# Other places for the buffers modulo 512 bytes, eight blocks of modulation weights later, and the last products in another order

## The chip, the cores and the metric

The kernel runs on one core of one Trainium2 chip, as one launch. The metric is the device time in microseconds (us). TensorE is called PE here, its weight load PEld, VectorE DVE, ScalarE ACT, GpSimd POOL, and the queue of SyncE, which issues the loads of the weights, SP.

## What is computed

Two blocks of a transformer follow each other on 256 tokens of width 1024, each with two layers, all in float32. Each layer is a mixer and a feed-forward part, and what goes into and out of both is scaled by rows that depend on the condition `c`.

```python
def swiglu(h, w1, w3, w2):
    a = jnp.einsum("btd,df->btf", h, w1)
    g = jnp.einsum("btd,df->btf", h, w3)
    return jnp.einsum("btf,fd->btd", jax.nn.silu(a) * g, w2)        # d = 1024, f = 2816
...
for layer in range(DEPTH):                                           # first block, DEPTH = 2
    shift, scale, gate = modulation(c, ada_w[layer, 0], ada_b[layer, 0])
    h = x * (1.0 + scale) + shift
    y = hybrid_mixer(h, ...)                                         # w_in, three small mixers, w_out
    x = layer_norm(DN_ALPHA * x + (1.0 + gate) * y, ...)
    shift, scale, gate = modulation(c, ada_w[layer, 1], ada_b[layer, 1])
    h = x * (1.0 + scale) + shift
    y = swiglu(h, ...) if layer % 2 == 0 else moe_swiglu(h, ...)     # 8 experts, top 2
    x = layer_norm(DN_ALPHA * x + (1.0 + gate) * y, ...)
...
for l in range(L):                                                   # second block, L = 2
    mod = (cond @ w_mod[l] + b_mod[l])[:, None, :]
    sh_a, sc_a, g_a, sh_f, sc_f, g_f = jnp.split(mod, N_MOD, axis=-1)
    h = rms_norm_2(x, norm_mix[l]) * (1 + sc_a) + sh_a
    ...                                                              # w_in, two kinds of attention
    x = x + g_a * (jnp.concatenate([o_m, o_d], axis=-1) @ w_out[l])
    h = rms_norm_2(x, norm_ffn[l]) * (1 + sc_f) + sh_f
    x = x + g_f * ((jax.nn.silu(h @ w_gate[l]) * (h @ w_up[l])) @ w_down[l])
```

## The kernel before

**Weights in blocks of 1 MB.** All large weights come in blocks of 128 partitions by 2048 float32 numbers, each one DMA of SP, into a ring of six slots (`ring`, NS = 6). `plan` is the list of the blocks in order. SP waits for a slot until the block that lay in it has been used. A feed-forward part has 33 blocks: 22 of w1 and w3 and 11 of w2. `weave` puts blocks of modulation weights (`mods`, four blocks for each of 24 pieces `(m, j)`: m is the part, j = 0, 1, 2 shift, scale and gate) between the others; `lead` and `tail` say how many blocks of the main list stay free of them at its start and end.

**Three products for one.** Each number is split into a high and a low half that PE multiplies as float32r. ACT makes the high half of a weight block (`high_halves`, `ring_hi`, L1293), DVE subtracts to get the low half into the slot itself (`low_halves`, `ring_lo`, L1990), and `product` (L510 to L513) issues three matmuls: high by high, high by low, low by high. In a row of the profile the names behind `bank<-` are first the moving operand, which streams through PE, then the stationary one, which is loaded as weights (128 columns, 512 bytes in each partition).

**Which operand is which.** In `up`, and in `feature_block` of the first mixers, the rows of activations `hh`, `hl` move (256 columns) and the weight block is stationary. In `token_block`, `project` and the output blocks it is the other way round: `hh`, `hl` (or `yl`) are stationary and the weight block moves, with 256 (168 in one block) or 512 columns. In `down` and `last_down` the units (`uh`, `ul`, which lie in `work`; in groups of odd number parts of `PTr`) are stationary and 512 columns of weights move. The eight experts run in the branch `moe_picked`: for each the picked rows are gathered into `hgh`, `hgl` (in `QK` for experts 0, 1, 3, 4, 6 and 7; for experts 2 and 5 in the buffer of `hT` and `hl`, so that the profile names it `hl`) and are stationary under 512 columns of weights, or 256 in an expert's last group.

**Modulation on DVE.** DVE multiplies and sums a modulation block in two instructions of 1024 columns (`gemv`, L1930). It does so inside `low_halves`, ahead of the split of the next block in the plan, so the place of a modulation block in the plan sets its place in DVE's order.

**The end of a feed-forward part.** `last_down` works on result blocks 9 and 10 (the last two of 11) over four output quarters `Y[t][hf]`. DVE takes each quarter as soon as its last product is done, and the next part's norm follows from there.

**Fillers.** `turn_over` issues matmuls on constants whose results nobody reads.

**Where the buffers lie.** Each buffer begins where the one before ends, at a multiple of 32 bytes. In the built program the ring begins at byte 16,512 of a partition, which is 128 modulo 512. All the buffers up to `PT` are multiples of 512 bytes long, so they begin at 128 as well: the ring, `ring_hi`, `X`, `hT`/`hl`, `hh`, `XN`, `YT`/`yl`, `PT`/`PTr`. `PT` is 17,216 bytes long, so `YK`, `QK` (with `hgh`, `hgl`), `acc`, the gates and `cst` begin at 448, and `work` (with `uh`, `ul`) at 416. Slices inside these buffers, as the products take them, are multiples of 512 bytes apart, except in the block of 168 columns.

Of the kernel before, what the change touches and what calls it, by code (L numbers as in the profile page):

```python
# [88 lines left out]
def hybrid_kernel(nc, a, out):  # L89
    ctx = ExitStack()  # L90
    with ctx:
# [19 lines left out]
        X = sb("X", [128, 2, 1024])  # L111
        hT, hl = sb_over("hT", [128, 8, 256], "hl")
        hh = sb("hh", [128, 8, 256], F32R)
        XN, xl = sb_over("XN", [128, 2, 1024], "xl")
        YT, yl = sb_over("YT", [128, 8, 256], "yl")
        PT, PTr = sb_over("PT", [128, 4304], "PTr")
        YK = sb("YK", [128, 2, 1024])
        at_qk = (nc.sbuf_base + 31) // 32 * 32
        QK = sb("QK", [128, 4, 4, 256])
        hgl2 = over("hgl", [128, 2, 8, 128], at_qk)  # L120
        hgh2 = over("hgh", [128, 2, 8, 128], at_qk + 8192)
        acc = sb("acc", [128, 3072])
        gate = [sb(f"gate{i}", [128, 1024]) for i in range(NG)]
# [3 lines left out]
        pB = sb("pB", [128, 36])  # L127
        pD = sb("pD", [128, 80])
# [4 lines left out]
        small = sb("small", [128, 2, 24])  # L133
        gmr = sb("gmr", [128, 2, 256])
# [5 lines left out]
        prmD = YKf[:, 896:1024]  # L140
        at_work = (nc.sbuf_base + 31) // 32 * 32
        work = sb("work", [128, 2560])
        Sm = work[:, 0:1536].rearrange("p (j c) -> p j c", j=4)
# [7 lines left out]
        pos = sb("pos", [128, 2], I32)  # L151
        rp2 = sb("rp2", [128, 2, 2, 8])
        mlaw = sb("mlaw", [128, 1280])
        rtr, rtl = sb_over("rtr", [128, 8, 8], "rtl")
        rth = sb("rth", [128, 8, 8], F32R)
        comb = sb("comb", [128, 2, 8])
        st2 = sb("st2", [128, 48])
        flag = sb("flag", [128, 1], I32)
        sstat = sb("sstat", [128, 96])
        lam = sb("lam", [128, 2])  # L160
# [183 lines left out]
        def put_blocks(blocks):  # L344
            for b in blocks:
                block(*b)
# [4 lines left out]
        for i, n in enumerate((0, 1, 1, 1, 1, 2, 2)):  # L351
# [7 lines left out]
        put_blocks(weave(ffn_blocks((("ffn", 0), a["ffn_w1"][0], a["ffn_w3"][0], a["ffn_w2"][0])),  # L359
                         mods((1, 2), (4, 0), (4, 1), (2, 0), (2, 1), (2, 2), (3, 0), (3, 1))))  # L360
        put_blocks(weave(win_blocks(1) + rowblocks(("wout", 1), a["w_out"][1]), mods((3, 2))))
        put_blocks(weave(ffn_blocks(*[(("moe", x), a["moe_w1"][0, x], a["moe_w3"][0, x], a["moe_w2"][0, x]) for x in range(8)]), mods((4, 2)), 6, 6))
# [25 lines left out]
        for m in range(8):  # L388
            for j in range(3):
# [5 lines left out]
                if j == 2 and m >= 6:  # L395
                    sums.setdefault(turn_of[("win2", 1, 8) if m == 6 else ("wout2", 1, 1)], []).append((m, j))
                    continue
# [81 lines left out]
        def tensor_program(pe):  # L479
# [205 lines left out]
            def last_down(s, key):  # L685

                for i in (9, 10):
                    if key[0] != "moe":
                        summed(turn_of[(*key, "w2", i)])
                for t in range(2):  # L690
                    for hf in range(2):
                        for i in (9, 10):
                            wh, wl = weights(s, *key, "w2", i)
                            g, h = divmod(i, 2)
                            if t == 0 and hf == 0:
                                pe.wait_ge(*at(s.part, *key, "u", g, h))
                            for c in range(2):
                                w = slice(1024 * c + 512 * hf, 1024 * c + 512 * hf + 512)
                                j, z = 2 * h + c, slice(128 * t, 128 * t + 128)
                                x = product(Y[t][hf][:, :], fuh[g % 2][:, j, z], ful[g % 2][:, j, z], wh[:, w], wl[:, w], False, i == 10 and c == 1)  # L700
                            names = [("use", s.part, (*key, "w2", i)), (s.part, *key, "down", i, 1)] if t and hf else []
                            if i == 10:
                                names.append((s.part, *key, "result", t, hf))
                            if names:
                                x.then_inc(*s.prod(*names))

# [478 lines left out]
            first_sum(0)  # L1185
            turn_over(Y[1][1][:, :], 20)
            first_sum(1)
# [1951 lines left out]
```

## Time and profile before

| | |
|---|---|
| three timed runs | 2095.27 us median (2092.81 to 2095.79) |
| the profiled execution | 2093.15 us, of which the span of the trace is 2091.3 us |
| PE busy | 1990.1 us (95%), 11776 matmuls |
| DVE busy | 1672.5 us (80%) |
| ACT busy | 1169.8 us (56%) |
| DMA | 554.41 MB, mean 265 GB/s |

Busy time is the time in which an engine has at least one instruction under way. Matmuls overlap, so what a matmul costs in a row of them is not its duration but the distance from its start to the next one's. The clock is the share of the full PE clock that was granted.

In order of time the span holds: the first mixer (from 37 us), the first feed-forward part (186 to 392), the second mixer (400 to 534, with the choice of the experts), the experts (541 to 1351), the third mixer (1372 to 1536), its feed-forward part (1540 to 1737), the fourth mixer (1744 to 1897) and the last feed-forward part (1900 to 2087).

### The profile page before, as it was taken

To read this page: it belongs to the slowest core of one execution; us is meant where nothing else is said; L and a number is where in the kernel's file an instruction comes from. 1 tells how busy PE (TensorE), PEld (TensorE's weight loads), DVE (VectorE), ACT (ScalarE), POOL (GpSimd) and SP (SyncE) were. 2 spreads that over 40 slices of the span, in tenths; PEclk is the share of its full clock that TensorE was granted. 3 is DMA by queue.
4 is the path that set the end of the run, shared out by engine and by line. 5 is a ranking of instruction groups with operands and counts; after the bars stand their busy time and mean duration, and the time that the engine had idled before them with its cause. 6 is when DMAs were issued, how large, how long until landed. Compare 5 with 4: busy or idle time off the path is not lost.

```text
span 2091.3 us, 28839 instructions
## 1 busy us (share of the span) xinstructions
PE 1990.1 (95%) x11776; PEld 1696.9 (81%) x11798; DVE 1672.5 (80%) x1753; ACT 1169.8 (56%) x1316; POOL 72.8 (3%) x121
## 2 busy tenths in 40 slices
PE   7999999999899999999999999898899999989999
PEld 6778899786678888887888888677689988869998
DVE  6778889887789898989889888878778887856444
ACT  3544434464677776777777777456444345654432
POOL 6001000000000000000000000000010000000000
PEclk8999999999999999999999999999899999999999
DMA  9855999645599999999999999824369994324552
GB/s 354 265 188 192 356 350 359 213 140 192 193 336 341 359 366 333 351 360 366 330 351 364 363 337 350 293 95 148 121 230 346 352 356 145 122 72 150 182 185 97
DMA packets 251211, 554.41 MB, mean 265 GB/s; under 512 B 10076, under 2 KB 75856, under 8 KB 251072
## 3 DMA queue, kind: packets, MB, share of 16 engines
q1 hardware_dynamic: 247252, 544.13, 73.7%
q0 software_dynamic: 3552, 8.29, 1.1%
q8 instruction: 96, 1.57, 0.3%
q14 instruction: 43, 0.35, 0.0%
q10 hardware_dynamic: 268, 0.07, 0.0%
HBM read 551.40 MB, written 1.05 MB: 264 GB/s over the span
## 4 chain that ended last, share of the span: by engine, by line
PE 71%; DVE 15%; ACT 7%; issue 4%; DMA 4%; SPq 0%; ACTq 0%; DVEq 0%
PE bank L511 21%; PE bank L513 21%; PE bank L512 21%; DVE ring_lo L1990 4%; ACT ring_hi L1293 3%; DVE acc L1930 2%; DMA ring<-in_ffn_w_dram 1%; PE bank L902 1%; PE bank L1110 1%; DVE work L2175 1%; DMA ring<-in_w_in_dram 1%; DMA ring<-in_ada_w_dram 1%; PE bank L539 1%; DMA ring<-in_w_gate_dram 1%; DVE st L2179 1%
## 5 line engine op out<-in xcount | busy, mean ns | idle before, releaser
L1990 DVE TENSOR_TENSOR ring_lo<-ring,ring_hi 128x2048 fp32r<-128x2048 f32 x417 | 949.2, 2285 | 251.6 <-ACT ring_hi L1293 248.9
L1293 ACT ACTIVATE ring_hi<-ring 128x2048 fp32r<-128x2048 f32 x417 | 794.8, 1912 | 473.7 <-PE bank L513 225.5
L511 PE MATMUL bank<-hh,ring_hi 128*128 128x256 f32 x1152 | 328.2, 285 | 9.8 <-DVE ring_lo L1990 8.0
L512 PE MATMUL bank<-hl,ring_hi 128*128 128x256 f32 x1152 | 326.1, 283 | 0.0
L513 PE MATMUL bank<-hh,ring_lo 128*128 128x256 f32 x1152 | 326.0, 283 | 0.0
L513 PE MATMUL bank<-ring_hi,hl 128*128 128x256 f32 (+2 forms) x768 | 236.0, 307 | 0.0
L511 PEld LDWEIGHTS bank<-hh,ring_hi 128*128 128x128 f32 x1152 | 220.9, 192 | 13.6 <-issue 7.0
L511 PE MATMUL bank<-ring_hi,hgh 128*128 128x512 f32 (+1 forms) x576 | 220.6, 383 | 7.4 <-DVE ring_lo L1990 3.0
L512 PEld LDWEIGHTS bank<-hl,ring_hi 128*128 128x128 f32 x1152 | 221.1, 192 | 0.9 <-issue 0.5
L513 PEld LDWEIGHTS bank<-hh,ring_lo 128*128 128x128 f32 x1152 | 221.0, 192 | 0.0
L511 PE MATMUL bank<-ring_hi,hh 128*128 128x256 f32 (+2 forms) x672 | 209.3, 311 | 11.8 <-DVE hl L2054 6.5
L513 PE MATMUL bank<-ring_hi,hgl 128*128 128x512 f32 (+1 forms) x576 | 216.4, 376 | 0.0
L512 PE MATMUL bank<-ring_lo,hgh 128*128 128x512 f32 (+1 forms) x576 | 216.3, 376 | 0.0
L511 PE MATMUL bank<-ring_hi,uh 128*128 128x512 f32 x496 | 199.5, 402 | 7.3 <-DVE ring_lo L1990 6.1
L512 PE MATMUL bank<-ring_lo,hh 128*128 128x256 f32 (+2 forms) x672 | 202.6, 302 | 0.0
L512 PE MATMUL bank<-ring_lo,uh 128*128 128x512 f32 x496 | 197.1, 397 | 0.0
L513 PE MATMUL bank<-ring_hi,ul 128*128 128x512 f32 x496 | 197.1, 397 | 0.0
L1930 DVE SCALAR_TENSOR_TENSOR acc<-ring,csil,acc 128x1024 f32<-128x1024 f32 x140 | 179.7, 1283 | 12.8 <-DMA ring<-in_ada_w_dram 6.8
L513 PEld LDWEIGHTS bank<-ring_hi,hl 128*128 128x128 f32 x768 | 148.4, 193 | 6.6
L511 PEld LDWEIGHTS bank<-ring_hi,hh 128*128 128x128 f32 x672 | 130.9, 195 | 25.8 <-issue 15.8
L511 PEld LDWEIGHTS bank<-ring_hi,hgh 128*128 128x128 f32 x576 | 108.2, 188 | 33.5 <-issue 6.6
L512 PEld LDWEIGHTS bank<-ring_lo,hh 128*128 128x128 f32 x672 | 131.1, 195 | 4.6 <-issue 0.7
(427 smaller groups left out, 2815.2 us busy)
## 6 DMA issues: line engine op xcount, KB each, us to landing
ring<-in_moe_w_dram SPq DMA_DIRECT2D x264, 1024.0 KB, 5.3
ring<-in_ada_w_dram SPq DMA_DIRECT2D x48, 1024.0 KB, 7.4
ring<-in_w_mod_dram SPq DMA_DIRECT2D x48, 1024.0 KB, 7.6
ring<-in_w_in_dram SPq DMA_DIRECT2D x40, 1024.0 KB, 5.5
ring<-in_ffn_w_dram SPq DMA_DIRECT2D x33, 1024.0 KB, 5.7
ring<-in_w_gate_dram SPq DMA_DIRECT2D x22, 1024.0 KB, 5.1
ring<-in_w_up_dram SPq DMA_DIRECT2D x22, 1024.0 KB, 5.3
ring<-in_w_down_dram SPq DMA_DIRECT2D x22, 1024.0 KB, 5.1
```

The source lines that it names most:

```text
L511: pe.matmul(ps, xh, wh, start=first, stop=False)
L512: pe.matmul(ps, xh, wl, start=False, stop=False)
L513: return pe.matmul(ps, xl, wh, start=False, stop=last)
L539: x = pe.matmul(R2.of("gatesum", 0, h)[:, :], bc(csil[:, 2 * p + k:2 * p + k + 1], [128, 128]), w[:, k, 512 * h:512 * h + 512], start=p == ...
L902: x = pe.matmul(Y[t][h][:, :], YT[:, 2 * i + k, 128 * t:128 * t + 128], w[:, c:c + 512], start=first and k == 0, stop=False)
L1110: x = pe.transpose(ps[:, 128 * c:128 * c + 128], U[:, 128 * c:128 * c + 128], ident)
L1293: act.activation(ring_hi[i % NH][:, 0:z], ring[n % NS][:, 0:z], ACT.Copy).then_inc(*s.hi(("hi", home(s, i), i)))
L1930: x = dve.scalar_tensor_tensor(v, w[:, k, :], csil[:, col:col + 1], v, ALU.mult, ALU.add)
L1990: dve.tensor_tensor(ring_lo[n % NS][:, 0:z], ring[n % NS][:, 0:z], hi, ALU.subtract).then_inc(*s.lo(("lo", home(s, i), i)))
L2175: dve.tensor_tensor(S, R.of(*A, "scores", i, c)[:, 0:384], mask, ALU.add).then_inc(*vec(("free", *A, "scores", i, c)))
L2179: dve.tensor_reduce(mx[:, 1:2], S[:, 128:384], AXX, ALU.max).then_inc(*vec())
```

## The change

1. The buffers are allocated in another order. `QK`, `work`, `YK`, `acc`, the gates and `cst` now begin at 128 modulo 512, as `XN`, `YT`, `PT` and the ring still do; `hh` and `hT`/`hl` begin at 320.
2. Modulation piece (3, 1), four blocks, moves from the first feed-forward part to the second mixer, and piece (7, 2), four blocks, from the third feed-forward part to the last; the sum of (7, 2) on PE (L580, four matmuls) moves with it from the fourth mixer into the last feed-forward part.
3. `last_down` does three of the four quarters of block 9 before it turns to block 10.
4. The filler in the first 40 us has 15 matmuls, not 20.

```diff
@@ buffers
-        hT, hl = sb_over("hT", [128, 8, 256], "hl")
-        hh = sb("hh", [128, 8, 256], F32R)
         XN, xl = sb_over("XN", [128, 2, 1024], "xl")
-        YT, yl = sb_over("YT", [128, 8, 256], "yl")
-        PT, PTr = sb_over("PT", [128, 4304], "PTr")
-        YK = sb("YK", [128, 2, 1024])
         at_qk = (nc.sbuf_base + 31) // 32 * 32
         QK = sb("QK", [128, 4, 4, 256])
...
+        at_work = (nc.sbuf_base + 31) // 32 * 32
+        work = sb("work", [128, 2560])
+        YT, yl = sb_over("YT", [128, 8, 256], "yl")
+        PT, PTr = sb_over("PT", [128, 4304], "PTr")
+        rtr, rtl = sb_over("rtr", [128, 8, 8], "rtl")
+        rp2 = sb("rp2", [128, 2, 2, 8])
+        hh = sb("hh", [128, 8, 256], F32R)
+        hT, hl = sb_over("hT", [128, 8, 256], "hl")
+        small = sb("small", [128, 2, 24])
...
+        YK = sb("YK", [128, 2, 1024])
         acc = sb("acc", [128, 3072])
...
@@ plan
-                         mods((1, 2), (4, 0), (4, 1), (2, 0), (2, 1), (2, 2), (3, 0), (3, 1))))
-        put_blocks(weave(win_blocks(1) + rowblocks(("wout", 1), a["w_out"][1]), mods((3, 2))))
+                         mods((1, 2), (4, 0), (4, 1), (2, 0), (2, 1), (2, 2), (3, 0))))
+        put_blocks(weave(win_blocks(1) + rowblocks(("wout", 1), a["w_out"][1]), mods((3, 1), (3, 2)), 2, 2))
...
-                             mods((5, 2), (6, 0), (6, 1), (6, 2), (7, 0), (7, 1), (7, 2)) if l == 0 else []))
+                             mods((5, 2), (6, 0), (6, 1), (6, 2), (7, 0), (7, 1)) if l == 0 else mods((7, 2)), 2, 1 if l == 0 else 12))
...
@@ last_down
-                for t in range(2):
-                    for hf in range(2):
-                        for i in (9, 10):
...
+                early = [(0, 0), (0, 1), (1, 0)]
+                for i, t, hf in [(9, *q) for q in early] + [(10, 0, 0), (10, 0, 1), (9, 1, 1), (10, 1, 0), (10, 1, 1)]:
...
@@ start
-            turn_over(Y[1][1][:, :], 20)
+            turn_over(Y[1][1][:, :], 15)
```

PE's order at the end of the first feed-forward part, before; each row stands for six products (its own and the five left out below it), block 9 has the units `uh` and block 10 those in `PTr`, and the bank gives the quarter:

```order
L511 MATMUL bank0<-ring_hi0,uh_62 128x512
...
L511 MATMUL bank0<-ring_hi1,PTr_58 128x512
...
L511 MATMUL bank1<-ring_hi0,uh_62 128x512
...
L511 MATMUL bank1<-ring_hi1,PTr_58 128x512
...
L511 MATMUL bank2<-ring_hi0,uh_62 128x512
...
L511 MATMUL bank2<-ring_hi1,PTr_58 128x512
...
L511 MATMUL bank3<-ring_hi0,uh_62 128x512
...
L511 MATMUL bank3<-ring_hi1,PTr_58 128x512
```

And now:

```order
L511 MATMUL bank0<-ring_hi0,uh_63 128x512
...
L511 MATMUL bank1<-ring_hi0,uh_63 128x512
...
L511 MATMUL bank2<-ring_hi0,uh_63 128x512
...
L511 MATMUL bank0<-ring_hi1,PTr_59 128x512
...
L511 MATMUL bank1<-ring_hi1,PTr_59 128x512
...
L511 MATMUL bank3<-ring_hi0,uh_63 128x512
...
L511 MATMUL bank2<-ring_hi1,PTr_59 128x512
...
L511 MATMUL bank3<-ring_hi1,PTr_59 128x512
```

Six products of block 9 stood ahead of the first that needs block 10; now eighteen do.

DVE's order in the second mixer, before, from the second half of the row norm on (`XN<-YT,pA,XN` is the convolution, `acc` a modulation block, `ring_lo` the split of a weight block):

```order
L2024 TENSOR_TENSOR X<-XN,QK 128x1024
L2026 TENSOR_TENSOR X<-X,QK 128x1024
L1990 TENSOR_TENSOR ring_lo_50<-ring,ring_hi 128x2048
L2237 SCALAR_TENSOR_TENSOR XN<-YT,pA,XN 128x256 x6
...
L1930 SCALAR_TENSOR_TENSOR acc<-ring,csil,acc 128x1024 x2
L1990 TENSOR_TENSOR ring_lo_52<-ring,ring_hi 128x2048
L2237 SCALAR_TENSOR_TENSOR XN<-YT,pA,XN 128x256 x6
L1990 TENSOR_TENSOR ring_lo_53<-ring,ring_hi 128x1344
L2237 SCALAR_TENSOR_TENSOR XN<-YT,pA,XN 128x256 x6
```

And now:

```order
L2023 TENSOR_TENSOR X<-XN,QK 128x1024
L2025 TENSOR_TENSOR X<-X,QK 128x1024
L1929 SCALAR_TENSOR_TENSOR acc<-ring,csil,acc 128x1024 x2
L1989 TENSOR_TENSOR ring_lo_53<-ring,ring_hi 128x2048
L2236 SCALAR_TENSOR_TENSOR XN<-YT,pA,XN 128x256 x6
...
L1929 SCALAR_TENSOR_TENSOR acc<-ring,csil,acc 128x1024 x2
L1989 TENSOR_TENSOR ring_lo_49<-ring,ring_hi 128x2048
L2236 SCALAR_TENSOR_TENSOR XN<-YT,pA,XN 128x256 x6
L1929 SCALAR_TENSOR_TENSOR acc<-ring,csil,acc 128x1024 x2
L1989 TENSOR_TENSOR ring_lo_51<-ring,ring_hi 128x1344
L2236 SCALAR_TENSOR_TENSOR XN<-YT,pA,XN 128x256 x6
```

Two more modulation blocks stand ahead of the splits of the fifth and the seventh input block. A third stands in the same way ahead of the eighth.

DVE's order at the end of the same mixer, before, ahead of the split of the output blocks:

```order
L2067 TENSOR_TENSOR yl<-YT,hh 128x512 x2
L1930 SCALAR_TENSOR_TENSOR acc<-ring,csil,acc 128x1024 x2
L1990 TENSOR_TENSOR ring_lo_54<-ring,ring_hi 128x2048
L1990 TENSOR_TENSOR ring_lo_49<-ring,ring_hi 128x2048
L1990 TENSOR_TENSOR ring_lo_50<-ring,ring_hi 128x2048
L2074 TENSOR_TENSOR XN<-bank,gate 128x512
```

And now:

```order
L2066 TENSOR_TENSOR yl<-YT,hh 128x512 x2
L1929 SCALAR_TENSOR_TENSOR acc<-ring,csil,acc 128x1024 x4
L1989 TENSOR_TENSOR ring_lo_54<-ring,ring_hi 128x2048
L1989 TENSOR_TENSOR ring_lo_49<-ring,ring_hi 128x2048
L1989 TENSOR_TENSOR ring_lo_50<-ring,ring_hi 128x2048
L2073 TENSOR_TENSOR XN<-bank,gate 128x512
```

The fourth extra block is summed here, so that four instructions of `acc` stand ahead of the split, not two.

## Rows read from the trace of the kernel before

**Rows 1.** The page, sections 1 and 4: busy time by engine; the chain of waits.

```profile
PE 1990.1 (95%) x11776; PEld 1696.9 (81%) x11798; DVE 1672.5 (80%) x1753; ACT 1169.8 (56%) x1316; POOL 72.8 (3%) x121
...
PE 71%; DVE 15%; ACT 7%; issue 4%; DMA 4%; SPq 0%; ACTq 0%; DVEq 0%
```

**Rows 2.** Windows over five stages: PE, PEld, DVE, ACT, POOL busy, clock, DMA, GB/s.

```profile
185.70:392.30 206.60, 198.60 (x1361) 183.68 (x1362) 181.53 (x142) 81.22 (x68) 6.71 (x10) 0.98 0.87 316
399.70:533.90 134.20, 125.55 (x846) 103.43 (x849) 105.59 (x208) 78.82 (x141) 6.60 (x10) 1.00 0.45 151
541.00:1351.00 810.00, 793.03 (x3740) 646.61 (x3741) 712.27 (x478) 573.92 (x427) 0.00 (x0) 1.00 0.98 347
1539.60:1737.30 197.70, 192.22 (x1327) 178.40 (x1326) 164.06 (x124) 81.32 (x70) 1.44 (x2) 0.99 0.87 314
1899.60:2087.00 187.40, 187.39 (x1320) 176.19 (x1320) 93.07 (x63) 75.10 (x59) 0.00 (x0) 1.00 0.47 155
```

**Rows 3.** Timeline of PE in the last feed-forward part: start, duration, instruction.

```profile
1945.78 0.40 PE L511 MATMUL bank<-ring_hi,uh 128*128 128x512 f32 x1
...
1956.97 0.28 PE L511 MATMUL bank<-hh,ring_hi 128*128 128x256 f32 x1
...
1980.00 0.40 PE L511 MATMUL bank<-ring_hi,PTr 128*128 128x512 f32 x1
...
1990.90 0.28 PE L511 MATMUL bank<-hh,ring_hi 128*128 128x256 f32 x1
```

**Rows 4.** Timeline of PE in the experts: 36 products with 256 columns, twice.

```profile
634.89 0.37 PE L511 MATMUL bank<-ring_hi,hgh 128*128 128x256 f32 x1
...
639.07 0.45 PE L511 MATMUL bank<-ring_hi,uh 128*128 128x512 f32 x1
...
834.71 0.36 PE L511 MATMUL bank<-ring_hi,hl 128*128 128x256 f32 x1
...
839.11 0.40 PE L511 MATMUL bank<-ring_hi,uh 128*128 128x512 f32 x1
```

**Rows 5.** Lines of PE by form: count, busy us, mean ns.

```profile
L511 PE MATMUL bank<-hh,ring_hi 128*128 128x256 f32 x1152 | 328.2, 285 | 9.8 <-DVE ring_lo L1990 8.0 <-ACT hT L1348 1.4 <-DVE hl L2054 0.3
L511 PE MATMUL bank<-ring_hi,uh 128*128 128x512 f32 x496 | 199.5, 402 | 7.3 <-DVE ring_lo L1990 6.1 <-DVE ul L2697 1.0
L511 PE MATMUL bank<-ring_hi,hgh 128*128 128x512 f32 x480 | 193.4, 403 | 7.4 <-DVE ring_lo L1990 3.0 <-DVE hgl L2648 1.8 <-ACT QK L1754 1.5
L511 PE MATMUL bank<-ring_hi,hh 128*128 128x256 f32 x544 | 159.6, 293 | 10.2 <-DVE hl L2054 6.5 <-DVE ring_lo L1990 3.0 <-ACT PT L1440 0.8
L511 PE MATMUL bank<-ring_hi,hl 128*128 128x512 f32 x160 | 64.1, 400 | 2.4 <-DVE ring_lo L1990 1.2 <-ACT QK L1754 1.1
L511 PE MATMUL bank<-ring_hi,hgh 128*128 128x256 f32 x96 | 27.2, 283 | 0.0
```

**Rows 6.** Timeline of PE before two last result blocks, then a window's clock.

```profile
379.72 0.79 PE L511 MATMUL bank<-ring_hi,PTr 128*128 128x512 f32 x1 [3.97 <-DVE ring_lo L1990]
...
1725.92 0.51 PE L511 MATMUL bank<-ring_hi,PTr 128*128 128x512 f32 x1 [3.21 <-DVE ring_lo L1990]
...
379.00:386.00 7.00, 6.28 (x15) 4.97 (x16) 6.90 (x7) 1.24 (x2) 0.00 (x0) 0.52 0.48 152
```

**Rows 7.** Timeline of DVE and PE at the end of the second mixer.

```profile
498.57 2.60 DVE L1930 SCALAR_TENSOR_TENSOR acc<-ring,csil,acc 128x1024 f32<-128x1024 f32 x2
501.09 4.49 DVE L1990 TENSOR_TENSOR ring_lo<-ring,ring_hi 128x2048 fp32r<-128x2048 f32 x2
...
503.52 0.47 PE L511 MATMUL bank<-ring_hi,hh 128*128 128x512 f32 x1 [1.43 <-DVE ring_lo L1990]
```

**Rows 8.** Who waited for whom in the experts; then the page's GB/s by slice.

```profile
ACT ring_hi L1293 <- PE bank L513: 154.0, 149, 2.9
ACT ring_hi L1293 <- DMA ring<-in_moe_w_dram: 2.1, 3, 0.9
...
GB/s 354 265 188 192 356 350 359 213 140 192 193 336 341 359 366 333 351 360 366 330 351 364 363 337 350 293 95 148 121 230 346 352 356 145 122 72 150 182 185 97
```

More of the change, by code:

```diff
@@ L121, in hybrid_kernel @@
         hgh2 = over("hgh", [128, 2, 8, 128], at_qk + 8192)
+        at_work = (nc.sbuf_base + 31) // 32 * 32
[7 more added lines that the diff above has]
+        small = sb("small", [128, 2, 24])
+        rth = sb("rth", [128, 8, 8], F32R)
+        st2 = sb("st2", [128, 48])
+        sstat = sb("sstat", [128, 96])
+        pD = sb("pD", [128, 80])
+        YK = sb("YK", [128, 2, 1024])
         acc = sb("acc", [128, 3072])
@@ L127, in hybrid_kernel @@
         pB = sb("pB", [128, 36])
-        pD = sb("pD", [128, 80])
         lnc = sb("lnc", [128, 8])
@@ L132, in hybrid_kernel @@
         csil = sb("csil", [128, 16])
-        small = sb("small", [128, 2, 24])
         gmr = sb("gmr", [128, 2, 256])
@@ L140, in hybrid_kernel @@
         prmD = YKf[:, 896:1024]
-        at_work = (nc.sbuf_base + 31) // 32 * 32
-        work = sb("work", [128, 2560])
         Sm = work[:, 0:1536].rearrange("p (j c) -> p j c", j=4)
@@ L151, in hybrid_kernel @@
         pos = sb("pos", [128, 2], I32)
-        rp2 = sb("rp2", [128, 2, 2, 8])
         mlaw = sb("mlaw", [128, 1280])
-        rtr, rtl = sb_over("rtr", [128, 8, 8], "rtl")
-        rth = sb("rth", [128, 8, 8], F32R)
         comb = sb("comb", [128, 2, 8])
-        st2 = sb("st2", [128, 48])
         flag = sb("flag", [128, 1], I32)
-        sstat = sb("sstat", [128, 96])
         lam = sb("lam", [128, 2])
@@ L395, in hybrid_kernel @@
                 if j == 2 and m >= 6:
-                    sums.setdefault(turn_of[("win2", 1, 8) if m == 6 else ("wout2", 1, 1)], []).append((m, j))
+                    sums.setdefault(turn_of["win2", 1, 8] if m == 6 else turn_of["ffn2", 1, "w1", 5, 0], []).append((m, j))
                     continue
@@ L689, in last_down @@
                         summed(turn_of[(*key, "w2", i)])
-                for t in range(2):
-                    for hf in range(2):
-                        for i in (9, 10):
[L693 to L705, printed above, removed]
+                early = [(0, 0), (0, 1), (1, 0)]
+                for i, t, hf in [(9, *q) for q in early] + [(10, 0, 0), (10, 0, 1), (9, 1, 1), (10, 1, 0), (10, 1, 1)]:
+                    wh, wl = weights(s, *key, "w2", i)
+                    g, h = divmod(i, 2)
+                    if t == 0 and hf == 0:
+                        pe.wait_ge(*at(s.part, *key, "u", g, h))
+                    for c in range(2):
+                        w = slice(1024 * c + 512 * hf, 1024 * c + 512 * hf + 512)
+                        j, z = 2 * h + c, slice(128 * t, 128 * t + 128)
+                        x = product(Y[t][hf][:, :], fuh[g % 2][:, j, z], ful[g % 2][:, j, z], wh[:, w], wl[:, w], False, i == 10 and c == 1)
+                    names = [("use", s.part, (*key, "w2", i)), (s.part, *key, "down", i, 1)] if t and hf else []
+                    if i == 10:
+                        names.append((s.part, *key, "result", t, hf))
+                    if names:
+                        x.then_inc(*s.prod(*names))
             def attention(A, heads):
```

## The prediction

> **What bounds the kernel now.** I read the page first. PE is busy 95% of the span, and the chain of waits lies on PE for 71% of it [rows 1], so what shortens a run of matmuls shortens the kernel, unless something waits right behind. Then the windows by stage [rows 2]. In the last feed-forward part PE is busy for all of its 187.4 us. The first has 206.6 - 198.6 = 8.0 us idle, the third 197.7 - 192.2 = 5.5, and in both DMA is busy 0.87 of the time. The experts are busy 793 of 810 us with DMA at 0.98. In the second mixer PE (125.6) and DVE (105.6) share 134.2 us. The timeline gives the pace, from the first matmul of a run to the first behind it [rows 3]: 48 matmuls with `uh` (at 416) as the stationary operand and 512 columns take 1956.97 - 1945.78 = 11.19 us, 233.1 ns each; 48 with `PTr` (128) take 1990.90 - 1980.00 = 10.90, 227.1 each; between them 192 with 256 columns of `hh` (128) over a weight block (128) take 23.03, 119.9 each. In the experts [rows 4] 36 matmuls of 256 columns with `hgh` at 448 take 4.18 us, 116.1 each, and the same 36 of an expert whose rows lie at 128 take 4.40, 122.2 each. So the place modulo 512 counts: at 512 columns the stationary operand wants 128 (6.0 ns less than at 416), at 256 columns it wants 448 (6.1 less than at 128). In both pairs the moving operand begins at 128.
>
> **The addresses, product by product.** Counts are those of one of the three products of a kind, times 3 [rows 5].
> Units, 416 to 128 under 512 columns: 496 x 3 = 1488 matmuls, of them 8 experts x 11 blocks x 4 x 3 = 1056 in the experts, 432 in three feed-forward parts. At 6.0 ns: 6.3 us and 2.6 us (0.9 a part).
> Gathered rows, 448 to 128: 480 x 3 = 1440 at 512 columns save 8.6 us; 96 x 3 = 288 at 256 columns lose 1.8. Experts 2 and 5 go from 128 to 320 (160 x 3 = 480 at 512 columns): between nothing and the 6.0 ns that 416 costs, 0 to +2.9 us; I take +1.1. The experts save 6.3 + 8.6 - 1.8 - 1.1 = 12.0.
> `hh`, `hl` as the moving operand, 128 to 320 over a weight block at 128, 256 columns: 1152 x 3 = 3456, of them 352 x 3 = 1056 in each feed-forward part and 288 in the first two mixers. No row has a moving operand at 320. What the cheap row has is a distance: moving 128, stationary 448, that is 192 modulo 512. Moving 320 over stationary 128 is again 192. If the distance decides, each saves 6.1 ns; if the stationary place alone does, nothing; and 6.1 more is the other end, since one such move did cost that at 512 columns. I take -6.1, the row with the same distance: 6.4 us a part, 19.3 for three, 1.8 in the mixers.
> `hh`, `hl` as the stationary operand at 320 (token and projection blocks): 544 x 3 = 1632, distance 320, in no row. Between -6.1 and +6.1 ns, 10 us either way; I take half the gain, -5.0 us.
>
> **What of that is on the path.** In the feed-forward parts all of it. In the mixers PE alternates with DVE and ACT: half of 1.8 + 5.0, so 3.4. In the experts ACT waits 154 us for PE to release a tile and 2.1 us for DMA [rows 8], so PE sets the pace there, but the loads are near. 268 blocks of 1.049 MB are 281 MB; at 366 GB/s, the best slice of the page [rows 8], they need 768 us against 810 now. There is room for 12 us; since DVE is busy 712 of 810 and gives PE hiccups, I take 85%: 10.2.
>
> **Modulation blocks.** The first feed-forward part loads 61 blocks, not 65. At its 316 to 359 GB/s four blocks are 12 to 13 us of DMA. It waits for loads (8.0 us idle), so its idle goes to about 1: -7.0. In the third part, 57 blocks for 61, 5.5 goes to about 1: -4.4. Both figures include step 3. In the last part four more loads find DMA 0.47 busy and DVE 93 of 187: nothing, and if that cover went, 4 x 2.6 = 10.4 us. The sum of (7, 2) is four matmuls on PE in one place or the other: nothing.
> The second mixer pays. Each block is two `acc` instructions, 2.60 us together [rows 7], four blocks 10.4 us on DVE, which was busy 105.6 of 134.2. One stands where PE waits already: PE got its low half at 503.52, with 1.43 us idle and DVE without a gap ahead of it [rows 7], so that one costs its full 2.6. The other three stand ahead of splits in the middle, behind them the convolution, the rotations and the softmax that PE needs; but there ACT and PE make DVE wait too. Bounds 0 and 7.8 for the three; I take 1.4, as 28 us of DVE's stage are idle. Sum +4.0. SP only issues four loads more, at DMA 0.45.
>
> **The last products.** PE waits 3.97 and 3.21 us for the low half of block 10 [rows 6], six matmuls into the end. Now eighteen stand ahead of it, 12 x 0.227 = 2.7 us more cover; that wait is part of the idle counted. After it 30 matmuls follow, not 42. The wait in the first part also pulls the clock down: granted 0.52 from 379 to 386 [rows 6], 42 matmuls at 1.2 GHz for most of 7 us, so about 3.4 us lost. With a wait of a microsecond I expect the clock to hold: -3.0. The quarters now come in two pairs, so DVE's norm ends a bit closer behind the last: -1.0 over two parts. Filler 20 to 15: DVE is late anyway there: 0.
>
> **Sum.** -19.3 (up) -2.6 (units in three parts) -3.4 (mixers) -10.2 (experts) -7.0 -4.4 (idle) -3.0 (clock) -1.0 (norm) +4.0 (second mixer) = -46.9. The profiled execution took 2093.15, 2.1 below the median of the runs. 2095.3 - 46.9 = 2048.4, so 2048.
>
> **Rivals.**
> A, the stationary place alone decides: nothing from `hh` at 320. Without 19.3 and 3.4 the gain is 24.2: 2071. For it: both pairs of rows change the stationary operand alone. Against: the sign turns between 256 and 512 columns, which a rule on the stationary operand by itself does not give.
> B, the gain in the experts is lost since DMA, at 0.98, or DVE, at 0.88, is late next, and the first part stays on its loads (3 us less gained): -46.9 + 13 = -34: 2061.
> C, the addresses do nothing: only idle, clock, norm and mixer remain, -11.4: 2084. For it nothing in the rows, against it [rows 3, 4].
> This is what the Trainium skill says, in "SBUF — State Buffer", section "Who interferes with whom": PE has two read ports, one for the moving operand and one for LDWEIGHTS, independent of each other, and "PE and ACT never wait on anyone". The trace disagrees: 233.1 against 227.1 ns with only the stationary buffer's place different.
> D, slower: `hh` at 320 costs 6.1 ns more, not less, in both of its roles. 3456 + 1632 = 5088 matmuls are +31.0 us. The rest gives 24.2, so +6.8: 2102. It decides from 24.2 / 5088 = 4.8 ns a matmul on. For it: at 512 columns leaving 128 did cost 6. Against: at 256 it gained.
>
> **How the numbers follow.** Forecast 0.64, A 0.16, B 0.11, C 0.03, D 0.06. The forecast's own range is 2038 to 2058 (second mixer 0 to 10, stationary role either way). The range has to reach A and B: 2036 to 2076 leaves out C, D and the forecast's lower edge. A measurement of this kernel can tell about 0.2%, 4 us, from no change. Only D is slower: 0.06. Between D and C a part of either could end within 4 us: 0.02, taken from C. Faster 0.92.
>
> **What would show it.** In the last feed-forward part: 192 up products in 22.0 us (114 ns) if I am right, 23.0 under A, 24.2 under D; every 48 result products in 10.9 us; the part 187.4 - 7.3 = 180 us long. The experts: `hgh` runs at 227 ns with 512 columns and 122 with 256; about 800 us long; ACT's wait for the experts' loads above 10 us would be B. First part: idle at most 2 us, clock 1.00 at its end. Second mixer: `acc` x4 ahead of the output blocks' splits and PE's wait there 4 us, not 1.43. I am wrong if `up` stays at 120, or if the second mixer takes over 8 us more.

## The result and the profile after

Four runs of the changed kernel took 2073.2 us in the median (2071.79 to 2075.66), four of the kernel before beside them 2094.04 (2091.84 to 2095.79). The ratio is 0.9902, 95% interval 0.9885 to 0.9919: 1.0% faster, 20.8 us. Forecast was a gain of 46.9. The sign was right and 2073.2 lies in the stated 2036 to 2076, near its far end and near rival A's 2071; the size was not right.

The page of after, the rows that answer to [rows 1]:

```profile
PE 1971.2 (95%) x11793; PEld 1687.0 (81%) x11793; DVE 1672.0 (81%) x1753; ACT 1170.6 (56%) x1316; POOL 72.0 (3%) x121
...
PE 70%; DVE 17%; ACT 7%; issue 4%; DMA 2%; SPq 0%; ACTq 0%; DVEq 0%
```

PE is busy 18.9 us less, as long as the span became shorter (2072.5 for 2091.3). DVE has more of the chain, 17% for 15. Windows of after (columns as in [rows 2]: PE, PEld, DVE, ACT, POOL busy, clock, DMA share, GB/s), from the first feed-forward part to the last in the same order, the second mixer cut where [rows 2] cuts it:

```profile
184.20:377.20 193.00, 190.66 (x1361) 177.46 (x1362) 166.90 (x125) 80.91 (x67) 6.72 (x10) 1.00 0.89 323
390.90:534.80 143.90, 128.30 (x851) 105.73 (x849) 114.94 (x215) 77.66 (x138) 6.55 (x10) 0.98 0.48 166
542.00:1341.00 799.00, 781.81 (x3736) 645.79 (x3736) 710.81 (x475) 571.95 (x425) 0.00 (x0) 1.00 0.98 351
1534.00:1720.90 186.90, 185.80 (x1327) 173.89 (x1326) 152.78 (x113) 80.56 (x66) 1.44 (x2) 1.00 0.86 312
1883.60:2068.20 184.60, 184.52 (x1324) 173.02 (x1324) 102.30 (x71) 76.23 (x61) 0.00 (x0) 1.00 0.53 180
```

The first part's idle fell from 8.0 to 2.3 us, the third's from 5.5 to 1.1. The first part now ends at 377.2 and the second mixer begins at 390.9, where before it was 392.3 and 399.7: a gap of 14 us stands where one of 8 was. The second mixer is 9.7 us longer, with DVE busy 9.4 us more and a clock of 0.98. The experts are 8.6 us shorter, at DMA 0.98 as before.

The last part, PE's timeline (start, duration), as [rows 3]: the start of 192 up products, the first result product behind them, the start of the next 192 and the first behind those.

```profile
1938.48 0.28 PE L511 MATMUL bank<-hh,ring_hi 128*128 128x256 f32 x1
...
1961.09 0.39 PE L511 MATMUL bank<-ring_hi,PTr 128*128 128x512 f32 x1
...
1971.97 0.28 PE L511 MATMUL bank<-hh,ring_hi 128*128 128x256 f32 x1
...
1994.59 0.39 PE L511 MATMUL bank<-ring_hi,uh 128*128 128x512 f32 x1
```

192 up products take 22.61 us, 117.8 ns each: neither the 114 of the forecast nor the 120 of rival A. The 48 result products take 10.88 us, 226.7 each, as forecast. But the first 384 up products of the same part (1883.61 to 1927.59) go at 114.5. So `up` has two paces in one trace, with the same operands at the same places. In the experts, as [rows 4], 36 products of 256 columns with `hgh` now at 128 take 4.40 us, 122.2 each, as forecast:

```profile
634.80 0.36 PE L511 MATMUL bank<-ring_hi,hgh 128*128 128x256 f32 x1
...
639.20 0.40 PE L511 MATMUL bank<-ring_hi,uh 128*128 128x512 f32 x1
```

The stages, in us, from the start of the first product of one to that of the next in the timeline of each kernel (a feed-forward part ends at its last result product, its gap reaches to the first product of what follows). The columns behind after are experiments of the next section. Each column is one execution, and single stages differ by a few us without a cause in the edit: after and fill_last1 (next section) have the same instructions up to the first part, which starts at 184.3 in one and at 188.2 in the other.

| | before | after | places_only | order_only | back31 | old_last | hh128 | hh448 | fill_r64 |
|---|---|---|---|---|---|---|---|---|---|
| start of the first part | 185.8 | 184.3 | 187.7 | 187.1 | 185.0 | 185.3 | 186.9 | 187.8 | 185.4 |
| first part | 206.2 | 192.6 | 203.3 | 194.6 | 201.4 | 194.5 | 194.2 | 192.3 | 191.9 |
| gap behind it | 7.7 | 14.0 | 7.7 | 13.7 | 11.3 | 8.0 | 13.6 | 13.1 | 13.3 |
| second mixer | 141.4 | 151.1 | 141.1 | 151.0 | 141.1 | 152.9 | 151.3 | 154.0 | 151.4 |
| experts | 806.9 | 798.3 | 798.4 | 806.9 | 798.5 | 798.8 | 798.2 | 799.4 | 798.1 |
| third part | 197.4 | 186.6 | 191.5 | 189.7 | 185.7 | 188.7 | 189.2 | 187.2 | 183.4 |
| last part | 187.4 | 184.5 | 184.2 | 189.1 | 186.0 | 184.5 | 188.3 | 186.1 | 183.9 |

### The profile page after: what moved, and what is told of

Same layout as the page of the kernel before. It is cut to its first block, busy times and chain, and to the rows that moved or that the text cites. A ratio compares the mean times of both kernels' runs of the same rounds, so it can differ in the third digit from the quotient of the medians.

```text
span 2072.5 us, 28850 instructions
## 1 busy us (share of the span) xinstructions
PE 1971.2 (95%) x11793; PEld 1687.0 (81%) x11793; DVE 1672.0 (81%) x1753; ACT 1170.6 (56%) x1316; POOL 72.0 (3%) x121
## 4 chain that ended last, share of the span: by engine, by line
PE 70%; DVE 17%; ACT 7%; issue 4%; DMA 2%; SPq 0%; ACTq 0%; DVEq 0%
PE bank L511 21%; PE bank L512 20%; PE bank L513 20%; DVE ring_lo L1989 5%; ACT ring_hi L1292 3%; DVE acc L1929 2%; PE bank L901 1%; DMA ring<-in_ada_w_dram 1%; PE bank L1109 1%; DVE XN L2073 1%; PE bank L539 1%; DVE work L2174 1%; DMA ring<-in_ffn_w_dram 1%; PE bank L593 1%; PE bank L498 1%
```

## The experiments

My theory after the result: the gain comes from the buffers' places alone; the order of the work is worth nothing in sum, since the gap behind the first part and the second mixer give back what the parts gain. The rival: the two halves add as they were forecast, each smaller. For `up`: the distance between the operands decides, but a run has two paces at this distance; the rival, that the moving operand at 320 has a pace of its own and something else in the kernel disturbs it.

**places_only.** The kernel before with the allocation of the changed one:

```diff
-        hT, hl = sb_over("hT", [128, 8, 256], "hl")
-        hh = sb("hh", [128, 8, 256], F32R)
...
+        rp2 = sb("rp2", [128, 2, 2, 8])
+        hh = sb("hh", [128, 8, 256], F32R)
+        hT, hl = sb_over("hT", [128, 8, 256], "hl")
```

> The kernel before with the buffers at the places of the changed kernel; blocks, last products and filler as before. By the trace of the changed kernel, `up` gains 2 to 3 ns a product, not 6.1, and the experts 9 us; with units and mixers that is 18 to 22 us: about 2074 when before is 2094, and the order of the work gave nothing. By the rival, that the order gave its 11 of idle and clock and the places the rest, 10: about 2084. If the prediction's own 6.1 ns were lost only through the new order, 2059.

2077.19 us, ratio 0.9922 (0.9906 to 0.9938): 16 us gained, somewhat less than I expected and far from 2059. The experts gain the whole 8.5 us, the third part 5.9, the last 3.2. The first part gains 2.9 though its up products are as fast as after's: PE still waits 4.41 us for the low half of block 10. ACT waits 97.1 us for loads in this part, so I take it that the part ends when the loads let it; no run shows that by itself.

**order_only.** The changed kernel with the allocation of before: the diff above the other way round.

> The changed kernel with the buffers at the places of before; modulation blocks, last products and filler as changed. Theory: what the first and third feed-forward part gain in idle (about 7 and 4) the second mixer (10 us lost) and the norms behind the parts give back: 2092 to 2096, nothing. Rival: the order gives 11: 2083.

2092.81 us, ratio 1.0 (0.999 to 1.0011). The order gives nothing. First part 11.7 us shorter, gap 6.0 longer, second mixer 9.6 longer, third part 7.7 shorter, last part 1.7 longer. 16 and 0 make 16 of the 21; the 4 or 5 left are within what the intervals allow. The stages do not show that the two halves help each other: in the first part with its gap they give 2.9 and 5.7 alone and 7.3 together. The difference lies in the start of the first part and in the third mixer, which scatter.

**back31.**

```diff
-                         mods((1, 2), (4, 0), (4, 1), (2, 0), (2, 1), (2, 2), (3, 0))))
-        put_blocks(weave(win_blocks(1) + rowblocks(("wout", 1), a["w_out"][1]), mods((3, 1), (3, 2)), 2, 2))
+                         mods((1, 2), (4, 0), (4, 1), (2, 0), (2, 1), (2, 2), (3, 0), (3, 1))))
+        put_blocks(weave(win_blocks(1) + rowblocks(("wout", 1), a["w_out"][1]), mods((3, 2))))
```

> The changed kernel with piece (3, 1), four modulation blocks, back in the first feed-forward part. Theory: the second mixer gets the 10 us back that it lost, since they are DVE's four blocks ahead of splits, and the first part pays about 5 in idle: 2068, with the second mixer 10 us shorter. Rival: the mixer is long because of the clock and of the places of the buffers: the mixer stays and the first part pays, 2078.

2070.89 us, ratio 0.9891 (0.9875 to 0.9907), against after's 0.9902: no difference that can be told. The second mixer is back at 141.1, so its four blocks cost 10.0 us there. The first part pays 8.8 (more than the 5 I expected), of which its gap gives 2.7 back. Moving the piece gained nothing that shows: first part, gap and second mixer take 357.7 us together in after and 353.8 in back31. Where the 10 us lie in after, PE's waits in the timeline (last column: idle before, and for whom):

```profile
418.73 0.58 PE L511 MATMUL bank<-hh,ring_hi 128*128 128x256 f32 x1 [4.10 <-DVE ring_lo L1989]
...
502.75 0.47 PE L511 MATMUL bank<-ring_hi,hh 128*128 128x512 f32 x1 [4.14 <-DVE ring_lo L1989]
```

In back31 these two are 1.78, with 0.72 at the row ahead of it, and 1.42:

```profile
415.67 0.39 PE L511 MATMUL bank<-hh,ring_hi 128*128 128x256 f32 x1 [0.72 <-DVE ring_lo L1989]
424.03 0.39 PE L511 MATMUL bank<-hh,ring_hi 128*128 128x256 f32 x1 [1.78 <-DVE ring_lo L1989]
...
501.18 0.47 PE L511 MATMUL bank<-ring_hi,hh 128*128 128x512 f32 x1 [1.42 <-DVE ring_lo L1989]
```

The clock behind the two waits in after (windows; the clock is the number ahead of the last two):

```profile
418.40:421.80 3.40, 3.07 (x14) 3.07 (x15) 3.22 (x9) 2.44 (x5) 0.00 (x0) 0.50 0.71 287
503.70:507.20 3.50, 3.50 (x10) 2.68 (x10) 3.31 (x2) 1.07 (x2) 0.00 (x0) 0.51 1.05 388
```

In back31 it was 1.00 over the whole mixer:

```profile
397.60:531.80 134.20, 124.97 (x852) 102.51 (x851) 105.57 (x209) 78.68 (x140) 6.54 (x10) 1.00 0.44 147
```

Waits: 4.10 + 4.14 for 0.72 + 1.78 + 1.42, 4.3 us more. Clock: 6.9 us at 1.2 GHz, 3.4 lost. That is 7.7 of the 10. The windows of the two mixers show where the rest lies: PE is busy 128.30 us for 124.97, 3.3 more, which is the clock, and idle 15.6 for 9.2, 6.4 more. Beside the waits above, the idle before L810 (for DVE) is 1.38 for 0.46, and 0.88 stands before L828 (for ACT YK), where back31 has none.

**old_last.** The changed kernel with `last_down` as before (the diff of the change, the other way round).

> The changed kernel with the last products in the order of before. Theory: PE waits 3 to 4 us again for the low half of block 10 in the first part, but DVE's norm, whose quarters then come one by one, ends 3 us closer behind PE's last product; together within 2 us of the changed kernel, 2072 to 2076. Rival: the new order was worth the whole wait and the clock behind it, 6 us or more: 2080.

2074.67 us, ratio 0.9911 (0.9893 to 0.9928): no difference to after. PE waited 2.07 us for block 10, not 3 to 4. The gap fell to 8.0, and the part and the mixer paid 1.9 and 1.8. DVE's timeline in after shows why PE's order is worth so little here: the low half of block 10 is done, then come the rows and four quarters with hardly a gap, and `hl`, for which the next product waits.

```profile
367.86 4.49 DVE L1989 TENSOR_TENSOR ring_lo<-ring,ring_hi 128x2048 fp32r<-128x2048 f32 x2 [2.27 <-ACT ring_hi L1292]
372.27 1.22 DVE L2023 TENSOR_TENSOR X<-XN,YK 128x1024 f32<-128x1024 f32 x1
...
374.67 0.68 DVE L2073 TENSOR_TENSOR XN<-bank,gate 128x512 f32<-128x512 f32 x1
...
382.19 0.69 DVE L2073 TENSOR_TENSOR XN<-bank,gate 128x512 f32<-128x512 f32 x1
...
388.82 1.30 DVE L2053 TENSOR_TENSOR hl<-hT,hh 128x512 fp32r<-128x512 f32 x2
```

PE is meanwhile done and waits, and then does its transposes and fillers at the low clock (PE's timeline, then the window):

```profile
377.14 3.73 PE L562 MATMUL bank<-cst,YT 128*128 128x128 f32 x32
382.33 0.88 PE L593 MATMUL bank<-cst,XN 128*128 128x128 f32 x6 [1.45 <-DVE XN L2016]
385.12 0.69 PE L593 MATMUL bank<-cst,XN 128*128 128x128 f32 x2 [1.91 <-ACT both L1320]
386.09 1.97 PE L593 MATMUL bank<-cst,XN 128*128 128x128 f32 x8 [0.29 <-DVE XN L2016]
387.86 3.50 PE L498 MATMUL bank<-cst 128*128 128x512 bf16 x8
```

```profile
384.20:391.00 6.80, 5.59 (x19) 3.20 (x19) 5.29 (x16) 4.03 (x10) 0.00 (x0) 0.51 0.00 0
```

From DVE's first instruction behind that low half to PE's next product are 390.92 - 372.27 = 18.7 us in after and 387.71 - 370.77 = 16.9 in old_last; before it was 399.74 - 381.78 = 18.0. DVE has hardly a gap in that stretch, which is 17 to 19 us in both orders of PE's products: it belongs to DVE, whatever PE has left to do.

**hh128.** The changed kernel with `hh` and `hT`/`hl` at 128, by pads; **hh448** the same at 448, with pads of 32 and 96 numbers. The diff of hh128:

```diff
+        sb("pad0", [128, 80])
         hh = sb("hh", [128, 8, 256], F32R)
         hT, hl = sb_over("hT", [128, 8, 256], "hl")
+        sb("pad2", [128, 48])
```

> The changed kernel with hh and hT/hl at 128 modulo 512, as before. `up` goes back from 117.8 to 119.9 ns and the 288 to 384 at 115 to 120: 3168 products, about 9 us; the stationary use of hh from 121 to 120, nothing. Theory, that hh at 320 gained only that: 2081. If places beside hh's make `up` faster, it stays at 118 and the time is 2073.

2082.3 us, ratio 0.9946 (0.9932 to 0.9959). `up` is back at 120 to 121 in nearly every run of the trace. So `hh` at 320, in both of its roles, is worth 9 us (4 to 5 either way), less than half of the 22.7 that I gave it (19.3 and the mixers' 3.4). The theory's number, 2081, was met.

> The changed kernel with hh and hT/hl at 448 modulo 512 instead of 320. If the distance decides, 448 over a block at 128 is a distance no row shows as moving operand, 114 to 120 ns. If the moving place alone decides, likewise open; as stationary operand hh at 448 under 256 columns has the row of the experts before, 116 against 121 now: 1632 products x 5 ns = 8 us less, of which half is on the path, 2069; under a rule that only the place modulo 128 (448 = 64 modulo 128) counts, up goes to 114 and the time to 2065.

2076.09 us, ratio 0.992 (0.9906 to 0.9933). Neither of my numbers. `up` goes at 117.8 in nearly all runs. The products with `hh` as the stationary operand and 256 columns did become faster, to 115.1 ns in the mean, start to start within a row of them at full clock (after 117.5, before 119.8), but the time shows nothing of it. It also shows that 320 and 448, 192 and 64 from 128 modulo 256, share the pace of 117.8.

**places_alone.** The core of the kernel, in which PE runs alone (the pair (m, t) gives the places of the moving and the stationary operand in steps of 64 bytes):

```python
every = [(m, t) for t in range(8) for m in range(8)]
...
for x, (mm, ss) in enumerate((("mh", "sh"), ("ml", "sh"), ("mh", "sl"))):
    pe.matmul(b[:, 0:256], room[ss][:, 16 * t + z:16 * t + z + 128], room[mm][:, 16 * m + c:16 * m + c + 256], start=x == 0, stop=x == 2)
```

> A kernel that computes nothing of the reference: PE alone runs rows of float32r products (high by high, high by low, low by high) with the moving and the stationary operand at every pair of the eight places 0, 64, ... 448 modulo 512, 36 with 256 columns and 18 with 512; then the same beside DVE and ACT at work on 2048 columns, then ten pairs beside them and loads of 1 MB. If the distance between the two operands decides, the pairs with equal distance take the same: moving 128, stationary 448 and moving 320, stationary 128 at 256 columns both 114 to 116 ns, equal places 120 to 122. If each operand's place counts by itself, rows and columns of the table add up, and moving 320 stays 118. If neither counts without other engines, the first table is flat and the second is not.

Three pairs from PE's timeline, products of 256 columns with the stationary operand at 128: the first and the last of 36 with the moving operand at 128, at 192, at 320.

```profile
105.84 0.28 PE L49 MATMUL bank<-room_mh,room_sh 128*128 128x256 f32 x1
...
110.03 0.28 PE L49 MATMUL bank<-room_mh,room_sl 128*128 128x256 f32 x1
110.14 0.28 PE L49 MATMUL bank<-room_mh,room_sh 128*128 128x256 f32 x1
...
114.27 0.28 PE L49 MATMUL bank<-room_mh,room_sl 128*128 128x256 f32 x1
...
118.66 0.28 PE L49 MATMUL bank<-room_mh,room_sh 128*128 128x256 f32 x1
...
122.64 0.28 PE L49 MATMUL bank<-room_mh,room_sl 128*128 128x256 f32 x1
```

35 steps in 4.18, 4.13 and 3.98 us (from the unrounded starts): 119.5, 117.9 and 113.7 ns. The whole table, by distance (moving less stationary, modulo 256), is

| distance | 512 columns | 256 columns |
|---|---|---|
| 0 | 227.8 (229.1 to 229.3 in four pairs) | 119.4 to 120.1 |
| 64 | 229.5 to 229.9 | 117.7 to 117.9, but 113.4 in the third stretch |
| 128 | 232.1 to 232.9 | 118.5 to 118.8 |
| 192 | 232.7 to 233.4 | 113.7 or 117.8 |

The distance decides, and it repeats after 256 bytes, not 512. The same table beside DVE and ACT at work differs by 0.1 ns at most, except in its first pair, which ran partly at the low clock. So the differences are there with no other engine at work; it isn't another engine that disturbs PE. But at 192 the pairs fall into two paces: with the stationary operand at 0, 128, 256 and 384 both such pairs had 113.7 (one of the two 114.3 at 128 and 384), at 64 and 320 both had 117.8, at 192 and 448 one each. In the third stretch, beside loads, 320 over 128 came first and had 113.5, and 128 over 320 right behind it, distance 64, which was 117.7 in the table, kept 113.4. So the pace isn't one of a pair. What I take from it is that a run keeps the pace it was entered with; loads are the other thing that differs between the two stretches, and entry_alone, which has none, tells them apart.

**entry_alone.**

Shortened, with comments of mine:

```python
wide(pe, 36)                      # as `down`: 512 columns, both operands at 128
for f in fills:
    filler(pe, *f)                # nothing, or 1 to 3 matmuls of 32 to 512 columns
narrow(pe, 48, far)               # as `up`: 256 columns, moving operand at 320, then 384, 192
```

> A kernel that computes nothing of the reference: PE alone runs 36 products with 512 columns (both operands at 128, as `down`), then 48 with 256 columns (as `up`), again and again, with the moving operand at 320, 384 or 192 and the stationary one at 128, and between the two nothing or a filler of 32 to 512 columns, float32r or bfloat16. Theory: at a distance of 64 or 192 modulo 256 a run has two paces that keep themselves up, 113.4 and 117.8 ns, and how it is entered decides; from `down` without a filler it is 117.8, as in the changed kernel, and one of the fillers turns it to 113.4. Rival: the two paces have to do with the places above 512 bytes or with the banks, and no filler changes the pace. At 384 (distance 0 modulo 256) 119.5 to 120 throughout. Behind these come pairs whose high and low halves lie at different distances: if each product goes by its own distance they take the mean of their classes.

Moving at 320. Without a filler: the first and the last of 48 products. Then with a float32r filler of 64 columns: the filler, the first product, and the one behind the 48.

```profile
38.28 0.28 PE L37 MATMUL bank<-room_mh,room_sh 128*128 128x256 f32 x1
...
43.81 0.28 PE L37 MATMUL bank<-room_mh,room_sl 128*128 128x256 f32 x1
...
177.24 0.19 PE L51 MATMUL bank<-room_mh,room_sh 128*128 128x64 f32 x1
177.27 0.36 PE L37 MATMUL bank<-room_mh,room_sh 128*128 128x256 f32 x1
...
182.81 0.39 PE L37 MATMUL bank<-room_mh,room_sh 128*128 128x512 f32 x1
```

47 steps in 5.53 us are 117.8 ns; 48 in 5.54 are 115.4 with the start, and 113.3 over the last 24. Of 14 fillers seven turned the pace at 320 (bfloat16: one of 256 or of 512 columns, two of 64 or of 128; float32r: one of 64 columns, and of 256 at distances 64 and 128), seven did not (bfloat16: one of 32, 64, 128 or 192 columns, three of 128; float32r: one of 128 or 256 at distance 0). At 384, distance 0, the pace stayed at 120. Entered straight from `down` it is 117.8: the changed kernel's case. At 192, distance 64, it is 117.8 without a filler too, but other fillers turned it: only three of bfloat16 with 128 columns (115.2 over all 48, 113.3 over the last 24) and the float32r one of 256 columns at distance 0 (113.4), which are two of the seven that did not at 320. The float32r one of 64 columns left it at 117.7 there. So no filler is the right one by itself, and what in the entry decides is not shown. Of 16 mixtures of halves at different distances none was faster than 113. (Three records are missing from this trace, those of the bfloat16 filler of 512 columns.) Loads are absent from this kernel, so they are not what sets the pace.

**fill_r64, fill_b64, fill_last1.** Can the kernel have that? In `up`, for the groups behind `down`:

```diff
+                    if g > 1 and n == "w1" and k == 0:
+                        pe.matmul(ban[0][:, 0:64], wh[:, 0, 0:128], wh[:, 0, 0:64], start=True, stop=True)
```

> The changed kernel with one float32r filler of 64 columns ahead of each run of up products that follows `down` (four groups in each of three parts). Theory, that the pace of `up` (117.8 ns behind `down`) is set by how the run is entered: these runs go at 113.4, 12 runs of 96 or 192, some 2100 products x 4.4 = 9 us less, filler 12 x 0.1 = 1 us: 2065, with the first part's share uncertain (loads), so 2063 to 2069. Rival, that the slow pace comes from something else in the kernel: 117.8 stays and the time is 2074.

fill_b64 has `turn_over(ban[0][:, 0:64], 2)` instead of the matmul:

> The same with two bfloat16 fillers of 64 columns in place of the one. Theory: alone these turned the pace to 113.4 as well; the same 2063 to 2069. If waits in the kernel shift the entry, one of the two kinds of filler may fail where the other does not. Rival: 2074.

fill_last1 is fill_r64 with the products of `last_down` in the old order for the first part:

> As with the one float32r filler, and the first feed-forward part ends with the last products in the order of before. Theory: the boundary behind that part falls from 14 to 8 us and the part and the mixer behind it pay 4 of it back, as with the old order alone: 2 us less than with the filler alone, 2063. Rival: the boundary is long because the part ends earlier, and stays: no change or 2 us more.

2067.89 us, ratio 0.9868 (0.9852 to 0.9885); 2068.22, 0.9861 (0.9842 to 0.988); 2069.73, 0.9877 (0.9861 to 0.9894). fill_r64 is 27 us faster than before and 5 faster than after, and 2063 to 2069 was expected; that fill_last1 should gain 2 more was wrong, or too small to see. The first part's gap fell to 7.7 there, but the part took 5.8 us more. PE's timeline of fill_r64 in the last part: filler, first up product, first result product behind 192.

```profile
1934.92 0.19 PE L656 MATMUL bank<-ring_hi 128*128 128x64 f32 x1
1934.95 0.36 PE L511 MATMUL bank<-hh,ring_hi 128*128 128x256 f32 x1
...
1956.81 0.39 PE L511 MATMUL bank<-ring_hi,PTr 128*128 128x512 f32 x1
```

21.86 us for 192, 113.9 each, where after took 22.61. Nine of the twelve runs behind a filler turned so, 2 of 4 in the first part, 4 of 4 in the third and 3 of 4 in the last: 1632 products at 3.9 ns less, 6.4 us. Two of the three that did not, the second group of the first part (22.70 us) and the last group of the last part, come behind a sum of modulation (L580). In fill_b64 the latter took 10.98 us for 96, 114.4 each, and the former stayed; so one kind did fail where the other did not, as I had thought possible. A run can also turn in its middle: in fill_b64 the 192 from 315.72 go at 117.8 up to the 48th and at 113.3 behind a delay of PE there. Against the gain of fill_r64, the first 384 of the last part were entered at 118.4 in this trace, 1.5 us lost, since no filler stands there.

## Why the prediction was right or wrong

By stage, from the table above:

| us | forecast | measured |
|---|---|---|
| first part and the gap behind it | -17.8 | -7.3 |
| second mixer | +4.0 | +9.7 |
| experts | -10.2 | -8.6 |
| third part and its gap | -12.2 | -10.3 |
| last part | -7.3 | -2.9 |
| the other mixers | -3.4 | +0.5 |
| sum | -46.9 | -18.9 |

**`up` at 320, -19.3: the rule was right, the size was not.** The step that failed is "I take -6.1, the row with the same distance": the term of 19.3 was mis-sized, and hh128 prices it, with the stationary role of `hh`, at 9. The distance does decide, as places_alone shows, and rival A is wrong: `up` did not stay at 120. But distance 192 has two paces, and [rows 4] showed only the faster. Behind `down`, where most runs of `up` stand, it is 117.8, so 2.1 ns were gained instead of 6.1; in after only the first 288 to 384 products of a part got 113 to 115 between waits, and in places_only and back31 the last part's 384 went at 118.3. The expensive end, rival D, had nothing in it. Rival A's number, 2071, was nearly that of the runs by luck, for another reason.

**Stationary `hh` at 320, the mixers' -3.4:** 128 over 320 is distance 64, 117.9 ns alone, 2 ns less than 120, and the products in the mixers got it: 119.8 before, 117.5 after. The first of 96 of them in the fourth mixer and the instruction behind them, before and after, are 11.59 and 11.40 us apart:

```profile
1770.81 0.36 PE L511 MATMUL bank<-ring_hi,hh 128*128 128x256 f32 x1
...
1782.40 0.82 PE L984 MATMUL bank<-cst,PT 128*128 128x128 f32 x6
...
1754.17 0.37 PE L511 MATMUL bank<-ring_hi,hh 128*128 128x256 f32 x1
...
1765.57 0.60 PE L983 MATMUL bank<-cst,PT 128*128 128x128 f32 x4
```

That is some 3.4 us of PE's time for all 1632, but the mixers did not get shorter: in places_only, where the places alone are changed, the second, third and fourth differ from before by -0.3, +1.1 and -0.4 us. The failed step is the half that I put on the path. The third mixer, 166.7 us for 164.6 in after, also had a clock of 0.92 for 0.94.

**Units and gathered rows** came to 8.6 us of the 10.2 forecast (12.0 x 0.85), 16% less: 227.8 for 233.4 ns in the table, 7.5 to 8.8 us in the experts in every kernel with the new places. ACT's wait for the experts' loads is 1.7 us, 2.1 before [rows 8], which is against rival B. What the Trainium skill says ("SBUF — State Buffer", "Who interferes with whom"), that PE's two ports are independent, is not the whole of it here: with no other engine at work the pace goes from 227.8 to 233.4 ns by the operands' distance alone. My prediction also set its rows against the sentence that PE never waits on anyone, which is about engines in each other's way at the ports; the rows say nothing on that, and the second table, the same to 0.1 ns beside DVE and ACT at work, agrees with it. Rival C is wrong by places_only.

**First part, -7.0 idle, -6.4 `up`, -3.0 clock: three gains for one end.** The idle did fall by 5.7. But the step that failed is to add them (17.8 with the units and the norm; 7.3 came), for behind the part DVE decides. The end of block 10's low half, counted from the start of the part, moved from 196.0 to 188.0 us, by 8.0, and to it DVE's 18 us are added. What PE gained beyond that became the gap of 14 us. The clock did not hold either: the fall went from 379 to 386 in the last products, to 384 to 391 among the transposes, around waits of 1.45 and 1.91 us. I had looked at the wait that went, and not at what DVE still had to do when PE was through.

**Second mixer, +4.0 against 9.7 (back31: 10.0):** the wait at the output blocks is 4.14, as forecast, but 1.7 us of clock behind it were not in the sum. The three blocks in the middle, taken at 1.4, cost about 5, of which 1.7 are clock: one stands ahead of a split for which PE then waits 4.10, and each of the two waits takes the clock down for 3.4 us. "28 us of DVE's stage are idle" was no cover. My criterion, over 8 us, had named this.

**Third part:** idle to 1.1, as forecast. The norm behind it was to end closer, by 0.5; its gap grew instead, from 7.7 to 8.3 us, and order_only and back31 have 8.2 and 8.3 there, places_only and old_last 7.7, so it is the new order of the last products that lengthens it.

**Last part:** 384 products at 5.7 ns and 672 at 2.1, and the units' 0.9, are 4.5. Against them stands the sum of (7, 2) between `down` and `up`, 1.88 us long; the last part of order_only, which has it and the old places, is 1.7 us longer than before:

```profile
2038.97 1.88 PE L580 MATMUL bank<-acc,cst 128*128 128x512 f32 x4
```

The fourth mixer, from which it came, is no shorter in after, 154.7 us for 154.8. But its clock was lower, and where that was equal PE was busy 1.8 us less and the mixer 1.8 us shorter. Windows of it in before, after, places_only (the sum still in it) and fill_r64 (the sum moved):

```profile
1744.80:1899.60 154.80, 143.14 (x989) 123.96 (x995) 109.56 (x210) 89.26 (x184) 0.00 (x0) 0.98 0.33 109
1728.90:1883.60 154.70, 143.73 (x990) 124.40 (x991) 109.44 (x210) 88.44 (x182) 0.00 (x0) 0.96 0.33 109
1730.20:1884.60 154.40, 142.88 (x994) 122.89 (x995) 109.55 (x210) 89.30 (x184) 0.00 (x0) 0.98 0.33 110
1726.00:1878.60 152.60, 141.06 (x991) 121.87 (x991) 109.33 (x210) 88.32 (x182) 0.00 (x0) 0.98 0.34 111
```

So "four matmuls on PE in one place or the other: nothing" holds for the sum of both stages, as far as single traces tell; it was no reason to give the last part the whole 7.3, and the clock of the fourth mixer took what the mixer gained.

## What to carry to other kernels

Rows of float32r products have a pace that depends on the distance of their two operands: read it start to start, and lay buffers so that 512 columns run at distance 0 modulo 256. At 256 columns distances 64 and 192 have two paces, so read both of them and try a filler ahead of the row. Before gains of a stage are added, ask which engine is last at its end: a stage that ends on a load or on DVE's chain takes only one of them. Work moved into a stage with idle engines costs what it delays, and a wait of 4 us may cost the clock on top.

## What was unexpected of the hardware

The same row of matmuls, operands and places has two stable paces, 113.4 and 117.8 ns, at distances 64 and 192, and keeps the one it is entered with until PE is delayed, with no other engine at work too. One matmul of 64 columns ahead of it chose the faster with the moving operand at 320 and not with it at 192, where other fillers did. Why that is I can't say: no record shows what sets it. What makes the first run of a part enter at 114.5 in some traces and at 118.4 in others is open as well. At 256 columns the best distance is the one that is worst at 512.
